# Attention B's transfers and divisions ordered by slot, maxima and projections spread over the last gate points, and a longer alternation of the gates' banks

## The reference, cut to what matters

```python
q = (rms_norm(c_q) @ w_uq).reshape(B, S, 8, 96)
kv = (rms_norm(c_kv) @ w_ukv).reshape(B, S, 8, 64 + 64)     # k_nope, v
k = concat([k_nope, k_rope for every head])
q, k = rms_norm(q), rms_norm(k); rotary on the last 32
s = where(key_chunk <= q_chunk, q @ k^T * 96**-0.5, -inf)   # chunks of 64
y_B = softmax(s) @ v                                        # 8 heads of 64
m = sigmoid(gate_A) * (y_A @ W_branch_A) + sigmoid(gate_B) * (y_B @ W_branch_B)
x = x + m @ W_out
x = x + relu(rms_norm(x) @ W_ff1)**2 @ W_ff2
```

## Time and profile before

| | |
|---|---|
| median of 3 runs | 1480.18 us (1479.58 to 1483.08) |
| profiled execution | 1484.96 us |
| its span in the profile | 1483.2 us |
| PE / DVE / ACT / POOL busy | 1426.6 (96%) / 539.3 (36%) / 367.8 (25%) / 526.0 (35%) us |
| mean granted clock of PE | 0.988 |
| chain that ended last | PE 81%, DVE 6%, DMA 5%, POOL 3%, ACT 2%, issue 2% |
| gates | 127 to 389 us |
| attention B | 394 to 596 us |
| branches, W_out, feed-forward | 596 to 1483 us |

### The profile page before, as it was taken

One profiled execution on the slowest core, in us unless ns is written; L12 is line 12 of the kernel. 1 busy time (PEld: TensorE's weight loads), 2 busy tenths in 40 slices (PEclk: granted clock), 3 DMA queues, 4 the chain that ended last, 5 costly groups with the idle time before them and its releaser, 6 DMA issues.

```text
span 1483.2 us, 17278 instructions
## 1 busy us (share of the span) xinstructions
PE 1426.6 (96%) x6792; PEld 1164.7 (79%) x6792; DVE 539.3 (36%) x947; ACT 367.8 (25%) x811; POOL 526.0 (35%) x381
## 2 busy tenths in 40 slices
PE   6999999999889998999999999999999999999998
PEld 6998776777666655888888888888888888888887
DVE  5302715633566764346253213122222212222222
ACT  5113225642245544101033012030210202011020
POOL 2333723436085420244308043150613315051320
PEclk9999999999999998999999999999999999999999
DMA  7121221210102011734203011020201202021112
GB/s 230 31 58 43 75 88 38 75 58 29 38 5 49 12 15 12 248 100 185 71 1 100 29 58 57 28 71 14 85 28 45 68 13 86 14 71 42 35 35 99
DMA packets 98105, 90.45 MB, mean 61 GB/s; under 512 B 21376, under 2 KB 84352, under 8 KB 98048
## 3 DMA queue, kind: packets, MB, share of 16 engines
q1 hardware_dynamic: 97904, 89.17, 19.7%
q10 hardware_dynamic: 144, 0.52, 0.1%
HBM read 76.99 MB, written 12.62 MB: 60 GB/s over the span
## 4 chain that ended last, share of the span: by engine, by line
PE 81%; DVE 6%; DMA 5%; POOL 3%; ACT 2%; issue 2%; SPq 0%; DVEq 0%; ACTq 0%; POOLq 0%
PE PS L1245 73%; DMA r_row<-r_store 3%; PE PS L1439 2%; PE PS L1252 1%; DMA r_store<-b_rsum 1%; PE PS L1389 1%; DVE uT_lo L1962 1%; PE PS L1338 1%; DVE b_part L1823 1%; PE PS L1375 1%; PE PS L1360 1%; ACT gate L1048 1%; DVE y_raw L1842 1%; PE PS L1403 1%; POOL b_rstd L781 1%
## 5 line engine op out<-in xcount | busy, mean ns | idle before, releaser
L772 POOL TENSOR_SCALAR w_hi<-raw 128x1024 fp32r<-128x1024 f32 x64 | 74.2, 1160 | 408.0 <-PE PS L1245 406.7
L1962 DVE TENSOR_TENSOR uT_lo<-relu_sq,uT_hi 128x512 fp32r<-128x512 f32 x64 | 92.0, 1473 | 278.9 <-ACT uT_hi L1233 278.9
L1219 ACT ACTIVATE relu_t<-PS 128x512 f32<-128x512 f32 x64 | 34.8, 595 | 553.3 <-PE PS L1245 553.3
L1968 DVE TENSOR_TENSOR xr<-PS,xr 128x1024 f32<-128x1024 f32 x64 | 78.3, 1224 | 245.7 <-PE PS L1245 245.7
L774 POOL TENSOR_TENSOR w_lo<-raw,w_hi 128x1024 fp32r<-128x1024 f32 x64 | 159.4, 2491 | 5.3
L1245 PE MATMUL PS<-mT_hi,w_hi 128*128 128x512 f32 x512 | 160.5, 390 | 0.7 <-POOL w_lo L774 0.7
L1245 PE MATMUL PS<-mT_hi,w_lo 128*128 128x512 f32 x512 | 160.3, 389 | 0.0
L1245 PE MATMUL PS<-mT_lo,w_hi 128*128 128x512 f32 x512 | 160.2, 389 | 0.0
L1245 PE MATMUL PS<-w_hi,uT_hi 128*128 128x512 f32 x512 | 158.5, 391 | 1.7 <-DVE uT_lo L1962 1.7
L1245 PE MATMUL PS<-w_lo,uT_hi 128*128 128x512 f32 x512 | 157.7, 389 | 0.0
L1245 PE MATMUL PS<-w_hi,uT_lo 128*128 128x512 f32 x512 | 157.7, 389 | 0.0
(11 more groups left out here) (208 smaller groups left out, 2425.8 us busy)
## 6 DMA issues: line engine op xcount, KB each, us to landing
raw<-in_w_ff SPq DMA_DIRECT2D x64, 512.0 KB, 3.8
g_raw<-in_w_in SPq DMA_DIRECT2D x16, 512.0 KB, 4.0
gate_store<-gate SPq DMA_DIRECT2D x16, 512.0 KB, 2.6
x_in<-in_x SPq DMA_DIRECT2D x8, 512.0 KB, 10.5
gate_a<-gate_store SPq DMA_DIRECT2D x8, 512.0 KB, 6.8
gate_b<-gate_store SPq DMA_DIRECT2D x8, 512.0 KB, 5.8
raw<-in_w_out SPq DMA_DIRECT2D x8, 512.0 KB, 3.5
xr<-in_x SPq DMA_DIRECT2D x8, 512.0 KB, 7.6
```

The costliest lines, as they stand in the source:

```text
L772: pool.tensor_scalar(hi_ap, raw_ap, 1.0, 1.0, ALU.mult, ALU.mult).then_inc(hi_done, 1)
L1219: act.activation(relu_t[:, cols], PS[:, 2 * (j % 2) + h, :], ACT.Relu).then_inc(relu_ready, 1)
L1962: dve.tensor_tensor(uT_lo[:, j, cols], relu_sq[:, cols], uT_hi[:, j, cols], ALU.subtract).then_inc(uT_ready, 1)
L1968: dve.tensor_tensor(xr[:, t, :], pair(4 + 2 * (t % 2)), xr[:, t, :], ALU.add).then_inc(x3_added, 1)
```

## The change

Six things, all of order and place. (1) Gate 5 too uses banks 0 and 1, and the small transposes take four banks in turn instead of six. (2) The turns of group 0 stand at points 55, 56, 58 and 59, the 12 chunks of head 0 at points 57, 58 and 60 to 63, two at each, and group 1's first four projections at points 60 to 63; its other four and its turns come earlier in head 0 (`FIRST`). The first four tiles wait only for the first half of the turns. (3) Group 1's values lie elsewhere, so the wait for the last gate moves to group 2. (4) SP moves head 0's maxima before the stores of gates 14 and 15, and in each head issues by slot: the maxima three, one, one, one, one, one, and between them the sums, the store of the reciprocals and their spread, which are now two procedures. (5) The reciprocal is taken at `block_end + 5`, y_norm at `+ 9`, y_high at `+ 9`, y_low at `+ 10`. (6) The two parts of a maximum are joined by a reduction instead of a minimum of two operands.

```diff
...
 PROJ_AT = 47
-TURN_AT = 56
-SHIFT_AT = 60
+TURNS = {55: (8, 9), 56: (10, 11), 58: (12, 13), 59: (14, 15)}
+SHIFTS = {57: (0, 1), 58: (2, 3), 60: (4, 5), 61: (6, 7), 62: (8, 9), 63: (10, 11)}
+SECOND = {60: (0,), 61: (1,), 62: (2,), 63: (3,)}
 SLOPES = [float(2.0 ** (-8.0 * (h + 1) / A_HEADS)) for h in range(A_HEADS)]
...
         rtmp = [place(f"rtmp{i}", 199.875 + 0.5 * i, [P, 4, B_GROUP, RH]) for i in range(4)]
-        vB = [place(f"vB{i}", (195.75, 62, 66.25)[i], [P, T, B_GROUP, V_DIM + 1]) for i in range(3)]
+        vB = [place(f"vB{i}", (195.75, 202, 66.25)[i], [P, T, B_GROUP, V_DIM + 1]) for i in range(3)]
         q_nat = place("q_nat", 177, [P, T, B_GROUP, QK])
...
-            return 0 if u in (1, 3) else 5
-        SMALL_BANKS = (0, 1, 2, 3, 4, 7)
+            return 0 if u in (1, 3, 5) else 5
+        SMALL_BANKS = (2, 3, 4, 7)
...
-            return SMALL_BANKS[n % 6]
+            return SMALL_BANKS[n % 4]
...
                 return [p - PROJ_AT]
-            if 0 <= p - TURN_AT < T // 2:
-                return [T + 2 * (p - TURN_AT), T + 2 * (p - TURN_AT) + 1]
-            return []
+            return list(TURNS.get(p, ()))
...
-            q = p - SHIFT_AT
-            return [3 * q, 3 * q + 1, 3 * q + 2] if 0 <= q < N_CHUNKS // 3 else []
+            return list(SHIFTS.get(p, ()))
+        def second_group(p):
+            return list(SECOND.get(p, ()))
...
         EVEN = (0, 1, 3, 4, 6, 7, 9, 10)
-        FIRST = (0, 1, 2, 2, 3, 3, 4, 5, 7, 8, 8, 9, 10, 10, 11, 11)
+        FIRST = (-1, -1, -1, -1, 0, 1, 2, 3, 5, 6, 6, 7, 9, 10, 10, 11)
...
             sp.dma_start(pos_row_i[:, :], positions[0:1, :].partition_broadcast(P)).then_inc(pos_landed, 16)
-            for u in range(2 * KD):
+            def gate_store(u):
                 sp.wait_ge(gate_ready, u + 1)
...
-            def nmax_move(u):
-                h, half = u // 2, u % 2
+            def nmax_move(h, *tiles):
                 with nc.allow_non_contiguous_dma(reason="128 numbers from a column to a row"):
-                    for i in range(Q_BLOCK):
-                        n = Q_BLOCK * half + i
+                    for n in tiles:
+                        half, i = n // Q_BLOCK, n % Q_BLOCK
                         if half == 0:
...
                             sp.wait_ge(nmax_ready, Q_BLOCK * h + i + 1)
-                        sp.dma_start(qT_hi[h % KQ_RING][QK:QK + 1, n * P:(n + 1) * P].bitcast(F32), b_nmax[:, u % 2, i:i + 1]
-                                     ).then_inc(nmax_landed[u % 2], 16)
+                        sp.dma_start(qT_hi[h % KQ_RING][QK:QK + 1, n * P:(n + 1) * P].bitcast(F32), b_nmax[:, half, i:i + 1]
+                                     ).then_inc(nmax_landed[half], 16)
+            for u in range(2 * KD - 2):
+                gate_store(u)
+            nmax_move(0, 0, 1, 2, 3)
+            gate_store(2 * KD - 2)
+            nmax_move(0, 4, 5, 6, 7)
+            gate_store(2 * KD - 1)
...
+            def reciprocal_store(u):
+                sp.wait_ge(rsum_b_ready, u + 1)
+                sp.dma_start(r_d[u % 2], b_rsum[:, u % 2, :]).then_inc(r_stored, 16)
             def reciprocal_spread(u):
                 s, r = u % 2, V_DIM * ((u // 2) % 2)
-                sp.wait_ge(rsum_b_ready, u + 1)
-                sp.dma_start(r_d[s], b_rsum[:, s, :]).then_inc(r_stored, 16)
                 sp.wait_ge(r_stored, 16 * (u + 1))
...
-            nmax_move(0)
-            nmax_move(1)
             for h in range(B_HEADS):
+                more = h + 1 < B_HEADS
                 if h < 2:
...
                         branch_load(e)
+                if more:
+                    nmax_move(h + 1, 0, 1, 2)
+                if h:
+                    sum_move(2 * h - 1)
+                if more:
+                    nmax_move(h + 1, 3)
+                if h:
+                    reciprocal_store(2 * h - 1)
+                if more:
+                    nmax_move(h + 1, 4)
+                if h:
+                    reciprocal_spread(2 * h - 1)
                 sum_move(2 * h)
-                if h + 1 < B_HEADS:
-                    nmax_move(2 * h + 2)
+                if more:
+                    nmax_move(h + 1, 5)
+                reciprocal_store(2 * h)
+                if more:
+                    nmax_move(h + 1, 6)
                 reciprocal_spread(2 * h)
-                if h + 1 < B_HEADS:
-                    nmax_move(2 * h + 3)
-                else:
-                    for b in range(2):
-                        sp.wait_ge(gate_stored[b], 16 * KD)
-                    sp.wait_ge(st_done, N_SLOTS)
-                    for d in range(3):
-                        fetch_a(d)
-                sum_move(2 * h + 1)
-                reciprocal_spread(2 * h + 1)
+                if more:
+                    nmax_move(h + 1, 7)
+            for b in range(2):
+                sp.wait_ge(gate_stored[b], 16 * KD)
+            sp.wait_ge(st_done, N_SLOTS)
+            for d in range(3):
+                fetch_a(d)
+            sum_move(BLOCKS - 1)
+            reciprocal_store(BLOCKS - 1)
+            reciprocal_spread(BLOCKS - 1)
             fetch_a(3)
...
                     group_act(0, q)
+                for q in second_group(p):
+                    group_act(1, q)
...
                         y_out(u)
-                    if t == block_end(u) + 7:
+                    if t == block_end(u) + 9:
                         y_high(u)
             y_out(BLOCKS - 1)
+            y_high(BLOCKS - 2)
             y_high(BLOCKS - 1)
...
                     pe.wait_ge(gate_ready, 4)
-                if n >= 6:
-                    wait_small_read(pe, n - 6)
+                if n >= 4:
+                    wait_small_read(pe, n - 4)
                 h = n // 6 if n < 12 else (n - 12) // 3
...
                 q, k = qT_hi[h % KQ_RING], kT_hi[h % KQ_RING]
-                if n == 0 and h % B_GROUP == 0:
-                    pe.wait_ge(qk_ready, T * (h // B_GROUP + 1))
+                if c == 0 and n % Q_BLOCK == 0 and h % B_GROUP == 0:
+                    pe.wait_ge(qk_ready, T * (h // B_GROUP) + (Q_BLOCK if n == 0 else T))
                 if a == 0:
...
                     approx(a)
+                for q in second_group(p):
+                    group_step(1, q)
             for t in range(N_SLOTS):
...
                         dve.wait_ge(bT_done, 8 * g)
-                    if p == 0 and g == 1:
+                    if p == 0 and g == 2:
                         dve.wait_ge(gate_done, 2 * KD)
...
                         dve.wait_ge(approx_read, a + 1)
-                        dve.tensor_tensor(out, b_part[:, n % 2, 0:1], b_part[:, n % 2, 1:2], ALU.min).then_inc(nmax_ready, 1)
+                        dve.tensor_reduce(out, b_part[:, n % 2, :], AX.X, ALU.min).then_inc(nmax_ready, 1)
...
                     row_max(a)
+                for q in second_group(p):
+                    group_vec(1, q)
             dve.wait_ge(gate_done, 2 * KD)
...
                 for u in range(BLOCKS):
-                    if t == block_end(u) + 4:
+                    if t == block_end(u) + 5:
                         sum_reciprocal(u)
-                    if t == block_end(u) + 6:
+                    if t == block_end(u) + 9:
                         y_norm(u)
-                    if t == block_end(u) + 8:
+                    if t == block_end(u) + 10:
                         y_low(u)
+            y_norm(BLOCKS - 2)
+            sum_reciprocal(BLOCKS - 1)
             y_low(BLOCKS - 2)
-            sum_reciprocal(BLOCKS - 1)
             y_norm(BLOCKS - 1)
...
```

## The result

| | before | changed |
|---|---|---|
| median | 1481.63 us (4 runs, 1479.58 to 1483.91) | 1460.85 us (4 runs, 1460.02 to 1461.41) |
| profiled execution, its span | 1484.96, 1483.2 us | 1460.02, 1458.2 us |
| mean granted clock | 0.988 | 0.996 |
| chain: PE, DVE, DMA | 81%, 6%, 5% | 86%, 6%, 1% |

The ratio is 0.9859, interval 0.9841 to 0.9878: 1.4% faster, 20.8 us between the medians. The forecast was 1455.2 in a range of 1448 to 1470.

What follows compares the result with a forecast made beforehand. TensorE bounds the kernel, losing idle time and granted clock in attention B. -0.9 (start) + 12.3 (head 0) + 23.5 (heads 1 to 7) - 9.9 = 25.0 us won: 1480.18 becomes 1455.2, range 1448 to 1470.

Steps and rivals of the forecast that it cites:

- the carried difference: Whole kernel: the median lay 4.8 us below the profiled execution, and this was carried over unchanged to the changed kernel.
- Gate banks: Gates 5 and 6: both waits of 0.42 us for the gate before to be read go, 0.84 us won.
- Last gate points: Points 55 to 63: chunks 0 and 1 hidden, chunks 2 and 3 cost 0.6; last gate ends near 388.4, +0.4 us.
- The sign of being wrong that I had named for this gap: Point 58, where PE waits for POOL: a half clock after it would show the forecast wrong.
- Start: Attention B: first scores wait for DVE's last two memsets, about 6.3 us after the last gate, 0.9 later than before.
- Head 0: Attention B: four projections (4.1), idle 6.3 and second slow stretch (1.9) go; 39.30 to 27.0 us, 12.3 won.
- the term given back: Heads 0 to 7: 9.9 us given back; 1.28 per head 0 to 4, 0.2 each in 5, 6, 3.1 in 7.
- Heads 1 to 7: Attention B: idle time 13.4 and ungranted clock 10.1 go, 23.5 us won, before the 9.9 given back.
- The slower rival: Chance 0.04: ACT's y_high waits for y_norm in the same slot, 15 blocks; slower from 1.7 us per block, 1493 at 2.5.
- The rival with DVE held by POOL: Chance 0.24: y_norm or y_low starts behind a POOL instruction in heads 0 to 4; 7 to 19 won, 1461 to 1473.
- The rival that y_norm comes late anyway: Chance 0.04: y_norm still comes late, waits meet in slot 9 and each gap only moves; 1476 to 1484 us.
- The reduction: Joining the two parts of a maximum on DVE: saves DVE a little, counted as nothing.

Runs made afterwards that it cites:

- experiments 5: The kernel before, unchanged, profiled a second time: median 1485.98 us, profiled execution 1480.89 us.
- experiment 6: The changed kernel repeated twice without edit: 1461.14 and 1461.37 us, beside 1480.96 and 1482.97 us of the kernel before.
- Experiment 8: The changed kernel with the first scores waiting for two memsets of ones only, the rest asked for at head 2: 1455.85 us.
- Experiment 7: The changed kernel with y_high and y_low each one slot later (10 and 11 after the block's end): 1455.43 us.
- experiment 10: The changed kernel with the two-operand minimum in place of the reduction: 1460.91 us.
- experiment 1: The changed kernel with the division's slots and SyncE's queue order of before: 1475.11 us.
- experiment 3: The changed kernel with the gates' bank pairs and six small banks of before: 1461.80 us.

## Why the prediction was right, and where it was not

**The step that failed is the carried difference.** The sum said 25.0 us less for the profiled execution, 1460.0; it was 1460.02. But I carried the 4.8 us between the profiled execution and the median over unchanged. It belonged to the kernel before, whose gaps and half clock differ from one execution to the next (experiments 5 and 6). The changed kernel scatters less, and its profiled execution is within 1 us of the median, 1460.85. That is the 5.6 us by which the forecast missed. The median of before was the right thing to compare with, and less of the ungranted clock should have been counted as won: held against the second profile of the kernel before, 1480.89 and the shortest of its ten runs, the gain is 20.9 and not 25.0.

**That the sum came out to the tenth is luck.** Its terms missed in both directions: the start by +1.9, head 0 by -1.5 and heads 1 to 7 by -0.5. Part of the first is a draw of the clock, as told below. The median is inside the forecast's own interval of 1449 to 1461 by 0.15 us.

**Gate banks**: right. The period of gate 5 went from 15.19 to 14.52 us. That is 0.67 for a wait of 0.42; a median can't tell 0.84 from 1.3 in all.

**Last gate points**: right in what they hid and cost. POOL held the turn of point 58 for 2.38 us (forecast 2.3):

```profile
365.56 1.05 PE L1279 MATMUL PS<-ident,q_nat 128*96 128x128 f32 x8 [2.38 <-POOL q_nat L907]
```

The sign of being wrong that I had named for this gap, a half clock behind it, is absent here but present in both repetitions (experiment 6).

The last gate ended near 386.6, 1.8 earlier than forecast. Most of that, 1.4, was there when point 60 began:

```profile
371.08 0.70 PE L1272 MATMUL PS<-hT_hi,gw_hi 128*128 128x512 f32 x2 [0.42 <-ACT gate L1072]
```

I had put 372.5. Of the rest of the way, the four points with two chunks and a projection each, only 0.4 came. The stretch before was shorter by more than the banks' 0.84: from the sigmoid of gate 7 to that of gate 8 the changed kernel took 1.05 us less (23.48 for 24.53), with the same gap and a clock of 0.89 in place of 0.79. That is not the change's work: the kernel before, profiled again, had 0.89 and took 23.20 there.

**Start**: right in mechanism, with the memsets as the last thing. PE and DVE in order of time:

```profile
391.84 0.91 DVE L1904 MEMSET kT_hi<- 1x1024 f32 x1 [0.16 <-issue]
...
392.81 0.80 PE L1446 MATMUL PS<-qT_hi,kT_hi 97*128 97x512 f32 x1 [4.56 <-DVE kT_hi L1904]
```

That is 6.2 us after the last gate (forecast 6.3), and 1.9 us before the 394.7, since the gate was early: +1.0 in place of -0.9.

**Head 0**: won 10.8 where 12.3 was said, or 11.0 with the 1.28 that the term given back holds for this head. I let the second slow stretch go (1.6 us of clock left), but the clock of the window is still 0.91, which is 2.6, and idle time of 1.0 remained. Experiment 8 shows that the gap at the start sets this clock: without it the head keeps 1.00.

**Heads 1 to 7**: 163.05 us became 149.95, 13.1 won, where 23.5 less 9.9 was said. Row by row that is 4.4 us less of idle time and 8.7 less of busy time: the 10.1 of ungranted clock, counted in full, gave 8.7. The idle time left in all heads, 9.9 us, is the size I gave back, but by another path. I had 1.28 for each of heads 0 to 4 as short waits for row maxima, and 3.1 in head 7. In the trace heads 1 and 3, where eight projections lie beside DVE, lose 0.3 and nothing, heads 2 and 4 lose 2.5 each and head 7 only 1.2, and most of it is one thing, y_high in the slot of y_norm. Experiment 7 took 5.0 of its 6.7 us away.

**The rivals.** The slower rival had named that very mechanism, and gave it 0.04 with a deciding point of 1.7 us per block. The mechanism was there and the price was not: PE lost 6.7 / 15 = 0.45 us per block. I should have charged it to the forecast as a term, and not kept it as a rival alone. The rival with DVE held by POOL was there too (1.48 us for 0.69), but here PE loses by it only where ACT waits. The Trainium skill (SBUF — State Buffer, section Who interferes with whom) has it so for a VectorE operation with two SBUF inputs beside a GpSimd one that reads SBUF, and on this chip never for a reduction. The lines of experiment 10 agree: 1310 against 156 ns at most. That rival's price was also worked out wrongly: 12 to 18 us lost of 25 leave 7 to 13 won, not 7 to 19, and POOL is not idle in head 5 (6.49 us). The rival that y_norm comes late anyway fell: DVE's wait for r_row went from 28.8 to 8.3 us (forecast under 12), with experiment 1 bringing it back to 32.9.

**The reduction**: worth nothing, as said, and shown by experiment 10.

## What to carry to other kernels

An operation that waits for a round trip over DRAM belongs as many slots behind its start as the trip takes in the trace, and its reader on another in-order engine belongs a slot behind that: a queue that stands for a late operand holds all that is behind it. When a kernel's long gaps go, count them once with their length and only partly with the clock; what the clock adds is a chance, and a single profiled execution shows one draw of it. Initial values that only later work reads should not stand ahead of the first work that waits.

## What the runs showed of the hardware

The same gap of 2.57 us before gate 8 went with a clock of 0.79 of full around it (232 to 248 us) in one execution of the kernel before and 0.89 in the other, with 0.89 in all three of the changed kernel, and with 1.00 in experiment 3. In the first profile a gap of 2.57 us also ends head 0, and head 1 behind it has the full clock. So a gap of this length brings the half clock often, but not always. What decides it is open; no run here tells.

The kernel before scattered over 1479 to 1491 us (over three chips; by up to 11.4 us on one in one job). The changed one, which keeps the three gaps named in experiment 6 but has none of over 2 us in heads 1 to 7, scattered over 1.6 us in three jobs. Which of the gaps makes the scatter is not shown.

A two-operand minimum of one column, 0.16 us by itself, took 1.31 us and ended with the POOL instruction beside it (422.24 and 422.22 us); the reduction that does the same work never took over 0.156 us in 32.
